# Samples' attention: scores one step behind the key transposes, keys copied by halves, one bank for the probabilities

## The reference, cut to what matters

```python
def gqa_attend(q, k, v, mask):
    s = jnp.einsum('bntgrd,bnsgd->bngrts', q, k) * ATT_SCALE
    p = masked_softmax(s, mask)
    return jnp.einsum('bngrts,bnsgd->bntgrd', p.astype(v.dtype), v), p
...
def nsa_sample(nq, kvc, kvs, kvw, ngate, pool_c, pool_s, win_buf, page_table):
...
    past_c = pool_c[page_table].reshape(B, PAST_LEN, 2, NSA_KV_HEADS, NSA_HD)
    kc = jnp.concatenate([block_means(past_c).astype(kvc.dtype), block_means(kvc)], axis=1)
    o_c, imp = compressed_branch(qg, kc, q_pos)
    n_sel = -(-(PAST_LEN + T) // SEL_BLOCK)
    idx, valid = select_blocks(imp, q_pos, n_sel)
...
    o_s = sel_attend(qg, kv_sel, idx, valid, q_pos)
    o_w, win_new = window_sample(qg, win_buf, kvw, q_pos)
    return nsa_combine(o_c, o_s, o_w, ngate), win_new
```

## Time and profile before

| | us |
|---|---|
| median of 3 runs | 1938.71 (1932.56 to 1940.87) |
| the profiled execution | 1931.92 |
| its span | 1930.1 |
| TensorE busy in the span | 1753.9 |
| samples' attention, first key transposes to last values | 855.1 to about 1227 |

### The profile page before, as it was taken

How to read it: one execution, slowest core, us unless ns; L and a number is a source line. 1 busy time by engine, 2 the same in 40 slices (tenths; PEclk the granted TensorE clock), 3 DMA queues, 4 the chain that set the end, 5 groups by cost and what they waited for, 6 DMA issues and landing times.

```text
span 1930.1 us, 25763 instructions
## 1 busy us (share of the span) xinstructions
PE 1753.9 (91%) x9667; PEld 1229.7 (64%) x9667; DVE 953.7 (49%) x1702; ACT 522.8 (27%) x1114; POOL 634.5 (33%) x634
## 2 busy tenths in 40 slices
PE   7999999989979799976788887998989999999996
PEld 6777777777857555653555555776467777763332
DVE  6767776672000367753454445233267777760003
ACT  3122222221010245533444445211222222220101
POOL 2344443431000322235565552141045556530000
PEclk9999999998979579988999999999989999999998
DMA  8677666664430100014776677432043232311111
GB/s 262 217 241 241 230 204 227 229 207 163 109 118 4 45 1 1 2 45 148 220 227 208 211 227 235 128 110 87 28 109 88 66 88 66 88 66 54 66 41 49
DMA packets 201014, 248.81 MB, mean 129 GB/s; under 512 B 32201, under 2 KB 173850, under 8 KB 192538
## 3 DMA queue, kind: packets, MB, share of 16 engines
q1 hardware_dynamic: 176684, 134.16, 23.8%
q0 software_dynamic: 21248, 109.46, 16.5%
q10 hardware_dynamic: 2960, 3.54, 0.5%
HBM read 236.09 MB, written 19.29 MB: 132 GB/s over the span
## 4 chain that ended last, share of the span: by engine, by line
PE 74%; DVE 11%; DMA 5%; issue 4%; ACT 3%; another core or an unknown queue 2%; ACTq 1%; SPq 0%; POOL 0%; DVEq 0%; POOLq 0%
PE ps L2118 21%; PE ps L2244 8%; PE ps L1735 7%; DVE mem L1247 4%; PE ps L2070 4%; PE ps L1746 4%; DMA mem<-in_cache_cmp_kv,pidx 4%; PE ps L2092 3%; PE ps L2183 3%; PE ps L2047 3%; PE ps L1767 3%; PE ps L1975 2%; PE ps L1996 2%; PE ps L1962 2%
## 5 line engine op out<-in xcount | busy, mean ns | idle before, releaser
L2118 PE MATMUL ps<-mem 128*128 128x288 f32 x1352 | 338.2, 408 | 0.8 <-DVE mem L1185 0.8
L2118 PEld LDWEIGHTS ps<-mem 128*128 128x128 f32 x1352 | 256.2, 191 | 70.7 <-DVE mem L1185 1.0
L734 POOL DMA_INDIRECT mem<-in_cache_sel_kv,sidx x192 | 186.1, 969 | 322.0 <-PE ps L1928 174.3
L1735 PE MATMUL ps<-mem 128*128 128x288 f32 x1024 | 269.7, 426 | 14.7 <-DVE mem L1273 13.6
L1735 PEld LDWEIGHTS ps<-mem 128*128 128x128 f32 x1024 | 203.6, 200 | 73.7 <-issue 14.6
L1247 DVE TENSOR_TENSOR mem<-mem 128x2048 f32<-128x2048 f32 x56 | 159.6, 2850 | 43.3 <-DMA mem<-in_cache_cmp_kv,pidx 42.7
L697 POOL DMA_INDIRECT mem<-in_cache_cmp_kv,pidx x56 | 90.4, 1615 | 239.5 <-DVE mem L1247 210.6
L2244 PE MATMUL ps<-mem 128*128 128x512 f32 x352 | 163.7, 608 | 0.0
L2092 PE MATMUL ps<-mem 128*64 128x512 f32 x288 | 83.3, 654 | 61.0 <-ACT mem L1032 35.9
L1519 DVE TENSOR_TENSOR mem<-ps,mem 128x512 f32<-128x512 f32 x64 | 44.3, 692 | 153.4 <-PE ps L2092 92.2
L2244 PEld LDWEIGHTS ps<-mem 128*128 128x128 f32 x352 | 63.9, 191 | 80.7 <-issue 80.6
(11 more groups left out here) (363 smaller groups left out, 2687.2 us busy)
## 6 DMA issues: line engine op xcount, KB each, us to landing
mem<-in_cache_sel_kv SPq DMA_DIRECT2D x320, 128.0 KB
mem<-in_w_up SPq DMA_DIRECT2D x44, 512.0 KB, 5.1
...
```

The lines of the kernel that those rows point to most:

```text
L734: pool.indirect_dma_start(kring[kq % NKR][:, j, :], None, pool_rows, bass.IndirectOffsetOnAxis(sidx[:, i:i + 1], 0)).then_inc(pg_g[kq % NK ...
L1735: mm = t.matmul(ps[:, 2 * (u % 2) + a, 0:NHF], lhs(k), hT[:, k, a * NHF:(a + 1) * NHF], start=(k == 0), stop=(k == KD - 1))
L2118: mm = t.matmul(ps[:, bank, 0:NHF], lhs[:, k, :], rhs[:, k, :], start=(first and k == 0), stop=(k == KD // 2 - 1), skip_group_check=True)
```

## The change

The scores of a step are no longer made in that step, behind the copy of its keys, but in the next one: `scores(s - 1)` stands at the end of step `s`, behind the key transposes of step `s`. For that the two halves of the transposed keys rotate through three banks (`KB` = 0, 1, 5), each half is transposed, reported (`ek_ok` counts halves now) and copied by itself, and there are three key buffers; the third lies in `avm` and `scanm`, which are free in this stage. The probabilities keep one bank, 4, where they had 4 and 5, so their transposes wait for the copy of the step before (`epT_ok` at `m` and not `m` − 1). `LAG` is 17. The exponentials, the softmax factors and the scaling of the sample before stand one step later (`c` = 1 to 4, 5, and 5 to 7); the selection of the next sample stands one or two steps earlier on TensorE (`c` = 1, 2, still 6 and 8), ScalarE (1, 4, 7) and VectorE (2, 4, 6, 8). `pscT` has three buffers. The hunks that are left out double counts of `ek_ok` and `ekT_ok` in the same way as the others.

```diff
@@ -76,7 +76,7 @@
 NC = NPC + 2
-LAG = NC + 6
+LAG = NC + 7
...
@@ -217,7 +217,9 @@
         ering += [view(PGC * KV).rearrange("p (g c) -> p g c", c=KV) for _ in range(NKR + NVR - len(ering))]
-        kTs = [view(2 * PGC * P).rearrange("p (g n) -> p g n", g=2) for _ in range(2)]
+        kTs = [[view(PGC * P) for _ in range(2)] for _ in range(2)]
+        kTs.append([avm[:, :, :, :].rearrange("p i r c -> p (i r c)"), scanm[:, 0:PGC * P]])
+        KB = (0, 1, 5)
...
@@ -226,7 +228,7 @@
         at[0] = a_vcz
-        psm, psg, pscT = view(P), view(P), [view(P) for _ in range(2)]
+        psm, psg, pscT = view(P), view(P), [view(P) for _ in range(2)] + [hmask[:, :]]
...
@@ -602,7 +604,7 @@
                     if kq >= KAHEAD:
-                        wait(sp, ek_ok, kq - NKR + 1)
+                        wait(sp, ek_ok, 2 * (kq - NKR + 1))
...
@@ -1000,9 +1002,9 @@
                 act.wait_ge(c7_ok, b + 1)
-                if b >= 2:
-                    act.wait_ge(epv_ok, NC * (b - 2) + 1)
-                a.activation(pscT[b % 2], cbank[:, 384:512], ACT.Copy).then_inc(c10_ok, 1)
+                if b >= 3:
+                    act.wait_ge(epv_ok, NC * (b - 3) + 1)
+                a.activation(pscT[b % 3], cbank[:, 384:512], ACT.Copy).then_inc(c10_ok, 1)
...
@@ -1025,31 +1027,32 @@
                     kq = b * (NPC + 1) + c
-                    act.wait_ge(ek_ok, kq + 1)
-                    if kq >= 2:
-                        bb, cc = divmod(kq - 2, NPC + 1)
+                    if kq >= 3:
+                        bb, cc = divmod(kq - 3, NPC + 1)
                         act.wait_ge(es_ok, NC * bb + cc + 1)
-                    a.activation(kTs[kq % 2], ps[:, 0:2, :], ACT.Copy).then_inc(ekT_ok, 1)
+                    for gp in range(2):
+                        act.wait_ge(ek_ok, 2 * kq + gp + 1)
+                        a.activation(kTs[kq % 3][gp], ps[:, KB[(2 * kq + gp) % 3], :], ACT.Copy).then_inc(ekT_ok, 1)
                 m = s - LAG
                 if m >= 0:
                     bb, cc = divmod(m, NC)
                     act.wait_ge(et_ok, m + 1)
                     wait(act, epv_ok, m - 1)
-                    src = ps[:, 4 + m % 2, :].rearrange("p (j q) -> p j q", q=P)
+                    src = ps[:, 4, :].rearrange("p (j q) -> p j q", q=P)
                     if cc < NC - 1:
                         ins = a.activation(pTs[m % 2], src, ACT.Copy)
                     else:
                         ins = a.activation(pTs[m % 2][0:S, 0:2, :], src[0:S, 0:2, :], ACT.Copy)
                     ins.then_inc(epT_ok, 1)
                 if b + 1 < SB:
-                    if c == 3:
+                    if c == 1:
                         e_c2(b + 1)
-                    if c == 5:
+                    if c == 4:
                         e_c5(b + 1)
                     if c == 7:
                         e_c7(b + 1)
-                if c < 4 and 0 < b <= SB:
-                    e_exp(b - 1, [c] if c < 3 else [3, 4])
+                if 1 <= c < 5 and 0 < b <= SB:
+                    e_exp(b - 1, [c - 1] if c < 4 else [3, 4])
...
@@ -1498,15 +1501,15 @@
                     e_out(m // NC)
-                if s == NC * SB + 7:
+                if s == NC * SB + 8:
                     dve.wait_ge(et_ok, NC * (SB - 1))
                     link(v.tensor_tensor(mtw[0], b12, b11, ALU.subtract))
-                if s == NC * SB + 8:
+                if s == NC * SB + 9:
                     v.tensor_tensor(mtw[1], b22, mtw[0], ALU.subtract).then_inc(mt_ok, 1)
-                if s == NC * SB + 9:
+                if s == NC * SB + 10:
                     v.tensor_tensor(mtw[2], b22, b12, ALU.subtract)
                     dve.wait_ge(mt_ok, 1)
-                if s == NC * SB + 10:
+                if s == NC * SB + 11:
...
@@ -1532,7 +1535,7 @@
                         v.tensor_reduce(x[:, 13:14], x[:, 10:12], AX.X, ALU.max, negate=True).then_inc(enm_ok, 1)
-                if c == 4 and 0 < b <= SB:
+                if c == 5 and 0 < b <= SB:
...
@@ -1540,16 +1543,16 @@
                     dve.wait_ge(ecf_ok, b)
-                if 4 <= c < 7 and 0 < b <= SB:
-                    e_scale(b - 1, ([0, 1], [2, 3], [4])[c - 4])
+                if 5 <= c < 8 and 0 < b <= SB:
+                    e_scale(b - 1, ([0, 1], [2, 3], [4])[c - 5])
                 if b + 1 < SB:
+                    if c == 2:
+                        e_c4(b + 1)
                     if c == 4:
-                        e_c4(b + 1)
-                    if c == 5:
                         e_c6(b + 1)
-                    if c == 7:
+                    if c == 6:
                         e_c8(b + 1)
-                    if c == 9:
+                    if c == 8:
...
@@ -2030,7 +2033,7 @@
                     for gp in range(2):
-                        t.matmul(obank[gp * S:(gp + 1) * S, 0:P], pscT[bb % 2][:, gp * S:(gp + 1) * S],
+                        t.matmul(obank[gp * S:(gp + 1) * S, 0:P], pscT[bb % 3][:, gp * S:(gp + 1) * S],
...
@@ -2047,6 +2050,21 @@
                 mm.then_inc(epv_ok, 1)
+
+            def scores(n):
+
+                b, c = divmod(n, NC)
+                kq = b * (NPC + 1) + c
+                wait(pe, esc_ok, n - 1)
+                for gp in range(2):
+                    out = ps[64 * gp:64 * gp + 64, 2 + n % 2, :]
+                    if c <= NPC:
+                        pe.wait_ge(ekT_ok, 2 * kq + gp + 1)
+                        mm = t.matmul(out, qbd[:, b, gp, :], kTs[kq % 3][gp], start=True, stop=True)
+                    else:
+                        for br in range(2):
+                            mm = t.matmul(out[:, br * S:(br + 1) * S], qbd[:, b, gp, :], kT[:, br, gp, T:N], start=True, stop=True)
+                mm.then_inc(es_ok, 1)
...
@@ -2064,40 +2082,31 @@
                     pe.wait_ge(pg_g[kq % NKR], gland[kq])
-                    wait(pe, ekT_ok, kq)
                     for gp in range(2):
+                        wait(pe, ekT_ok, 2 * kq + gp - 2)
+                        bank = KB[(2 * kq + gp) % 3]
                         for j in range(PGC):
-                            mm = t.transpose(ps[:, gp, j * P:(j + 1) * P], kring[kq % NKR][:, j, gp * P:(gp + 1) * P], ident[:, :])
-                    mm.then_inc(ek_ok, 1)
+                            mm = t.transpose(ps[:, bank, j * P:(j + 1) * P], kring[kq % NKR][:, j, gp * P:(gp + 1) * P], ident[:, :])
+                        mm.then_inc(ek_ok, 1)
                 if m >= 0:
                     pe.wait_ge(epn_ok, NP * bb + min(cc // 2, NP - 1) + 1)
-                    wait(pe, epT_ok, m - 1)
+                    wait(pe, epT_ok, m)
                     if cc < NC - 1:
                         o = cc * 512 if cc < NPC else SELW
                         for j in range(PGC):
-                            mm = t.transpose(ps[:, 4 + m % 2, j * P:(j + 1) * P], sc[bb % 2][:, o + j * P:o + (j + 1) * P], ident[:, :])
+                            mm = t.transpose(ps[:, 4, j * P:(j + 1) * P], sc[bb % 2][:, o + j * P:o + (j + 1) * P], ident[:, :])
                     else:
                         for j, o in enumerate((NPG * P, SELW + WIN)):
-                            mm = t.transpose(ps[0:S, 4 + m % 2, j * P:(j + 1) * P], sc[bb % 2][:, o:o + S], ident[:, :])
+                            mm = t.transpose(ps[0:S, 4, j * P:(j + 1) * P], sc[bb % 2][:, o:o + S], ident[:, :])
                     mm.then_inc(et_ok, 1)
                 if m >= 1:
                     e_values(m - 1)
-                if b < SB:
-                    wait(pe, esc_ok, s - 1)
-                    for gp in range(2):
-                        out = ps[64 * gp:64 * gp + 64, 2 + s % 2, :]
-                        if keys:
-                            if gp == 0:
-                                pe.wait_ge(ekT_ok, kq + 1)
-                            mm = t.matmul(out, qbd[:, b, gp, :], kTs[kq % 2][:, gp, :], start=True, stop=True)
-                        else:
-                            for br in range(2):
-                                mm = t.matmul(out[:, br * S:(br + 1) * S], qbd[:, b, gp, :], kT[:, br, gp, T:N], start=True, stop=True)
-                    mm.then_inc(es_ok, 1)
+                if 0 < s <= NC * SB:
+                    scores(s - 1)
                 if b + 1 < SB:
-                    if c == 3:
+                    if c == 1:
                         e_c1(b + 1)
-                    if c == 4:
+                    if c == 2:
```

6 lines of the change are left out of this document (3 added, 3 removed).

## The result

The changed kernel takes **1956.15 us** (7 runs, 1952.26 to 1961.09) beside 1938.71 us before (the same median over all 7 of its runs, 1932.56 to 1945.23): 1.0086 times as long, with a 95% interval of 1.0064 to 1.0108, or 17.4 us more. The forecast was 9 us less. The profiled execution has 1961.09 us with a span of 1959.4. Of its 29 us over the profiled one of before, 13 lie ahead of the stage, in work that the change doesn't touch, and 15.5 in the stage itself (387.6 us against 372.1).

What follows compares the result with a forecast made beforehand. It took TensorE as the bound, waiting mostly in front of the scores, with its reports late during gathers. Stretches −13, +1.4, +1.1 and tail +1.6 sum to −9 us: 1930 us, own range 1918 to 1946, overall 1900 to 1962.

Steps and rivals of the forecast that it cites:

- the base of 33.9 us: One sample's attention without waits, estimated from the last sample, which has no gathers left: 33.9 us.
- A: Step 7: TensorE's probability transposes wait for VectorE's scaling, 2.05 us a sample including 0.9 of lateness.
- B: Step 8: TensorE's new sum waits for VectorE's copy-out, 3.65 us plus 0.9 of lateness, 4.55 a sample.
- The clock: TensorE's lowered clock behind the new waits: 1.5 us a sample, bounds 0 to 3.4.
- Its own signs: Score waits near zero; waits of 1 to 3 us in step 7, 3.5 to 6 in step 8; other steps about 3.4.
- First stretch: Steps 0 to 15, only keys and scores: 56 us for 69.2, so −13, bounds −8 and −25.
- The four steps behind it: The second stretch's four steps besides its five samples, counted at 12.9 us of work.
- Third: Steps 70 to 78 and the transposes of 79, 33.1 us before: +1.1 us forecast.
- Tail: The end of the stage, one step more without key transposes and scores: +1.6 us.
- The single bank: Probability transposes wait for their copy: 0.7 us a sample; as a rival with later reports, 1965 us, chance 0.13.
- The score pair: Rival: the two score products no longer run side by side, 57 us on top, 1987 us; chance 0.06.
- The rival of reports on time: Reports nearly on time, clock at its higher level, bank and clock costing nothing: 1901 us, chance 0.25.

Runs made afterwards that it cites:

- e7: Changed kernel with VectorE writing the finished output earlier (step 6) and scaling before the scores in step 5, where reports come late: 1914.35 us, 0.9895 of the kernel before.
- e14: Changed kernel with GpSimd gathering two pages of four instead of three, no late reports: 1885.58 us, 0.9989 of the kernel before.
- e3: Changed kernel with VectorE writing the finished output earlier (step 6) and scaling before the scores in step 5, no late reports: 0.9842 of the kernel before.
- set 1: First group of follow-up runs, not one kernel: no trace has a late report, and the kernel before took 1888.9 us.
- e8: Changed kernel, unchanged, run again where reports come late: 1948.48 us, 1.0065 of the kernel before.
- e5: Changed kernel with both VectorE moves, plus two banks for key halves and two for probabilities again: 0.9924 of the kernel before.
- e13: Kernel before the change with GpSimd gathering two pages of four instead of three, no late reports: 1880.77 us, 0.9963 of the kernel before.

## Why the prediction was wrong

Two steps failed: the price of the clock behind the new waits, and the base of 33.9 us on which all terms were put. A sample was forecast at 33.9 + 2.05 + 4.55 + 0.7 + 1.5 = 42.7 us and took 47.0.

- **Terms A and B: right in place and near in sum.** Predicted 2.1 + 4.55 = 6.65 us a sample; the followed sample has 3.70 + 2.15 = 5.85, and from 940 to 1130 us the means are 2.8 and 2.7. They divide otherwise, and B stayed mostly below the 3.5 to 6 us that were to show it: the reports to VectorE are later than the 0.9 us taken (3.05 for the scores of step 5), which lengthens A, and while A lasts the output gets ready, which shortens B. Moving VectorE's two pieces removes both and brings 6.3 us a sample.
- **The clock: mis-sized.** It stood at 1.5 us a sample within bounds of 0 to 3.4. TensorE's idle time came out as forecast, 7.6 us against 6.6 + 0.7. Its busy time for the same products is 39.4 us, where it is 34.7 in the samples of before at a clock of 1.00 and 35.9 in those of e7 at 1.00: the lower clock costs 3.5 to 4.8 us, over the upper bound. That is 2.0 to 3.3 of the 4.3 us by which a sample missed. The step reasoned that the score waits, "which do it now, are gone": but those left the middle stretch at 0.98. Three of the five samples of before have the clock at 1.00 with 7 to 8 us of idle time in them, in waits of mostly 1 to 2 us, one of them 2.5. In the changed kernel all five samples are at 0.89 or less. Where exactly the line runs isn't shown: e14 had a wait of 3.53 us with the clock at 1.00 for over 20 us behind it.
- **The floor of 33.9 us holds only where reports are on time.** It was measured by TensorE's work in the last sample, which has no gathers, and e3 reached it to 0.1 us in set 1. Where reports are late, the same kernel takes 40.2, where the sum without A, B and the clock had 34.6. The prediction read the 4.64 us step in the earlier trace rows as TensorE waiting, and priced gathers at 3.76 us a step; GpSimd's own pause behind each group was not in it. So the lag of the scores, without A and B, is worth 1.7 to 3.1 us a sample (43.3 and 42.5 to 40.2; 35.7 to 34.0 where nothing is late) and not 8.6. By these runs the base was 5.6 us too low, and A, B and their clock together, forecast at 8.15 us, were worth 6.3 (e8 to e7). So the terms do not simply add; that the long waits hide a part of the lateness is the likely reason, and not shown.
- **Its own signs.** The score waits went, as said (0.8 us). Steps 0 to 6 were to follow in about 3.4 us; from 1039.82 to 1064.65 six of them took 4.1 each.
- **First stretch:** −17.4 us for a predicted −13, inside its bounds. **The four steps behind it:** 24.5 us for a predicted 16.3 (12.9 + 2.05 + 1.4). **Third:** +3.4 for +1.1; its clock was 0.95 for 1.00. **Tail:** −1.7 for +1.6.
- **The single bank** costs what was said, 0.7 us a sample: 4.4 us in 12 waits of the stage on the probability copy (L1043). The Trainium skill's "Perfetto Trace Analysis", section "Matmuls", would have independent groups rotate through banks; e5, which gives the second bank back and takes the third key bank away, is not faster.
- **The score pair** stays side by side: four records in 1.03 us, as before. The rival of reports on time took the clock as free and A and B at 5 us; where reports are on time (e13 and e14), the change still loses 4.2 us a sample.

Slower had 0.23, mostly for the single bank (1965 us), a time near the right one by a mechanism that didn't come. The 0.06 for the rest named one half of what came, that new waits take just what the old ones gave; no rival had the lower clock behind them.
